# Rows of 64 tokens by two picks in the second table pass, and part of the one-hot work moved beside the last rows

## The chip, the cores and the metric

One core of one Trainium2 chip runs the kernel. The metric is the device time of one execution in microseconds (us). Three executions of the kernel before took 2889.9, 2887.84 and 2890.3 us, median 2889.9. Engines: TensorE (PE, and PEld for its weight loads), VectorE (DVE), ScalarE (ACT), GpSimd (POOL), SyncE (SP, which issues transfers only).

## The reference

Two transformer blocks over 256 tokens of width 2048, all in float32. The change touches only the last step of the second one, a product-key expert layer:

```
def peer_ffn(h, w_q, sub_keys, expert_u, expert_v):
    scores = einsum('bshpd,hpnd->bshpn', q, sub_keys)      # q = h @ w_q, 8 heads x 2 halves
    sv, si = top_k(scores, 16)                             # 16 best keys of each half
    cand = sv[..., 0, :, None] + sv[..., 1, None, :]       # 256 sums, of which the 16 best
    tv, tp = top_k(cand, 16)                               # name 16 experts of 16384
    eidx, gw = ..., softmax(tv)
    a = einsum('td,ted->te', x, expert_u[eidx])            # 128 dot products of each token
    a = gelu(a) * gw
    out = einsum('te,ted->td', a, expert_v[eidx])          # weighted sum of 128 rows
```

So each of the 256 tokens picks 8 x 16 = 128 experts, reads 128 rows of the first table (`expert_u`, 8 KB a row), and adds up 128 rows of the second (`expert_v`).

## The kernel before, in words

The tokens stand in two blocks of 128, one token per partition; `tk` is 0 or 1. One "row" of the kernel is one pick of all 128 tokens of a block: an indirect transfer by POOL (line 624) that brings 128 table rows, 1 MB, into one slot of SBUF. There are 256 of them, n = 0 to 127 for the first block and 128 to 255 for the second. This is the row stage.

**The row stage.** Rows land in the slots of `aring` (4) and `ring` (4); `ROW_SLOT` and `ROW_BEFORE` (lines 246 to 253) name each row's slot and the row that must have left it; from n = 128 on there are 8. POOL waits for that row (line 618 to 622) and issues the next. Most rows are dotted on DVE (`dot`, line 2692) with the tokens in `sq`. 47 rows are dotted on PE (`TURN_EARLY`, every 4th from 30 to 142; `TURN_LATE`, every 5th from 144 to 229): `turn_and_dot` transposes the row in 16 pieces into M (line 1283), ACT copies M to `acc` in two halves (`keep_row`, line 1767), and PE multiplies the copy by the turned tokens (line 1293). DVE reads the diagonal of the product (`read_diagonal`, line 2702); in its written order this stands behind the dot of row n + 8 for a late row n (`READ_BEHIND`), and DVE waits there if PE is not done. DVE also picks the experts in 57 parts spread between the dots (`PICK_AT`).

**The one-hot groups.** The upper half of `expert_v` is not gathered but read whole, in 64 blocks of 1 MB, and multiplied on PE by a dense matrix `mix[tk]` of coefficients (the dense stage, line 1331). `mix` is made in groups of 4 tokens, 32 groups for each block. For the first block ACT makes a group (`one_hots` in the ACT part, lines 1743, 1748, 1751: 8 + 1 + 4 instructions), PE multiplies (`spread_coefs`, line 1271) and ACT copies the product into `mix[0]` (`keep_mix`, line 1757). These 32 groups stand between the late PE rows: `spreads_after` gives 28 of them to the 18 rows 144 to 229, one or two behind each row, and the last row has four more. PE and ACT both run in this written order, so a late PE row does not start before the groups of the row ahead of it are through. For the second block the coefficients are ready only when all rows are dotted; `mix[1]` lies where `ring` and `aring` are. Its one-hots are made by DVE (`one_hots`, line 2730), weighed by ACT (line 1809), multiplied by PE and kept by ACT. Two are made ahead (`MARKED_AT`).

**The burst.** Behind row 255: gelu, coefficients, their transpose, then 32 groups of `mix[1]`, on DVE each followed by one `v_add`: the lower half of `expert_v` is gathered by POOL (line 636, 256 transfers of 0.5 MB) and added by DVE with the coefficient (line 2720), except 8 rows of `V_ON_PE` and the last 4 of `V_LAST_ON_PE`, which PE adds.

**The dense stage.** PE multiplies 64 blocks, each 8 products for two `tk` and two halves, loaded by SP into three buffers as PE frees them; beside it POOL and DVE go on with the gathered rows. DVE ends the first dense half at n = 242 (`DENSE_OUT`), the second at n = 254, and the gathered half last.

The functions that the diff touches, with the line numbers of the profile:

## Time and profile before

| | |
|---|---|
| Median of 3 runs | 2889.9 us (2887.84 to 2890.3) |
| Profiled execution: time, span | 2892.87 us, 2891.1 us |
| PE, DVE, ACT, POOL busy | 2627.9, 2138.4, 621.4, 911.1 us |
| Moved by the DMA engines | 935.10 MB, mean 323 GB/s |
| Mean granted TensorE clock | 0.948 of 2.4 GHz |

The profile shows one execution, taken by the hardware profiler. "Idle before" an instruction names what released it, inferred from semaphores. A line such as L1283 is that line of the kernel. In rows of transfers "DMA ring<-peer_u" is the wait for that transfer to land. Busy time of PE is modelled at its ends, and the busy time of POOL is rough.

### The profile page before, as it was taken

The page shows a single profiled execution, that of the slowest core. Times are in us where ns is not written, and L with a number is a line of the kernel's source. Part 1 is how long each engine was busy: PE and PEld are TensorE (multiplying, and loading weights), DVE is VectorE, ACT ScalarE, POOL GpSimd, SP SyncE. Part 2 cuts the span into 40 slices and gives each one's busy share as a digit, 9 for nine tenths or more (in the row PEclk, how much of TensorE's full clock was granted, in tenths as well). Part 3 has the DMA queues.
Part 4 walks back from the last instruction along what each step waited for, and adds up shares of the span by engine and source line. Part 5 has one row for each costly group of instructions (what it writes and reads, how often), then busy time and mean ns, then how long its engine had stood idle before and what let it go on. Part 6 is the DMA issues. An engine that isn't in the chain of part 4 may idle for free.

```text
span 2891.1 us, 30550 instructions
## 1 busy us (share of the span) xinstructions
PE 2627.9 (91%) x11608; PEld 2038.4 (71%) x11608; DVE 2138.4 (74%) x2836; ACT 621.4 (21%) x1328; POOL 911.1 (32%) x712
## 2 busy tenths in 40 slices
PE   7999999999999999999999998776676648999998
PEld 6888778855687787578657687666666635666665
DVE  6797476697896757425677778989999888656666
ACT  1121240300100210121000221221477765000000
POOL 1100001000010100000000036767677676666664
PEclk9999999999999999999999999888877759999999
DMA  9954469888787743325878789999999998999998
GB/s 403 421 223 146 175 241 411 352 305 348 277 336 302 292 145 136 142 102 222 347 274 321 278 352 417 421 421 415 413 421 412 399 352 296 408 415 414 413 414 357
DMA packets 147734, 935.10 MB, mean 323 GB/s; under 512 B 16400, under 2 KB 16656, under 8 KB 53136
## 3 DMA queue, kind: packets, MB, share of 16 engines
q0 software_dynamic: 101376, 604.02, 52.3%
q1 hardware_dynamic: 44784, 320.66, 28.6%
q10 hardware_dynamic: 1440, 8.59, 0.7%
q8 instruction: 88, 1.44, 0.2%
q14 instruction: 46, 0.38, 0.0%
HBM read 929.02 MB, written 4.19 MB: 323 GB/s over the span
## 4 chain that ended last, share of the span: by engine, by line
PE 67%; DVE 11%; DMA 9%; ACT 6%; POOL 4%; issue 3%; DVEq 0%; SPq 0%; POOLq 0%
PE G L652 30%; PE M L1331 14%; PE M L979 6%; DMA aring<-peer_u,proj 3%; PE B L979 3%; ACT vec L1743 2%; DVE aring L2692 2%; POOL ring L624 2%; PE M L1283 2%; PE G L979 2%; POOL aring L624 2%; DMA aring<-ada 1%; PE G L1271 1%; PE M L893 1%; ACT vec L1748 1%
## 5 line engine op out<-in xcount | busy, mean ns | idle before, releaser
L652 PE MATMUL G<-h,ring 128*128 128x256 f32 x2784 | 610.2, 380 | 0.0
L652 PEld LDWEIGHTS G<-h,ring 128*128 128x128 f32 x2784 | 527.4, 190 | 79.3 <-issue 6.7
L609 POOL DMA_DIRECT2D aring<-ada x176 | 93.1, 529 | 1445.5 <-DVE mods L1879 1399.9
L1879 DVE CUSTOM_DVE_ANT_0 aring<-aring,acc,vec 128x2048 f32<-128x2048 f32 x160 | 372.4, 2351 | 57.5 <-DMA aring<-ada 54.5
L652 PE MATMUL G<-proj,ring 128*128 128x256 f32 x1472 | 322.1, 380 | 1.0 <-DVE proj L2515 0.9
L652 PEld LDWEIGHTS G<-proj,ring 128*128 128x128 f32 x1472 | 279.7, 191 | 41.4 <-issue 3.2
L1331 PE MATMUL M<-sq,mix 128*128 128x512 f32 x688 | 301.6, 594 | 1.2 <-DMA sq<-v_blocks 1.2
L624 POOL DMA_INDIRECT aring<-peer_u,proj x131 | 229.9, 1755 | 155.8 <-DVE proj L2645 51.8
L2692 DVE CUSTOM_DVE_ANT_0 aring<-sq,aring 128x2048 f32<-128x2048 f32 x107 | 244.1, 2291 | 36.2 <-DMA aring<-peer_u,proj 35.0
L1331 PEld LDWEIGHTS M<-sq,mix 128*128 128x128 f32 x688 | 203.5, 297 | 91.0 <-DMA sq<-v_blocks 2.0
L2720 DVE SCALAR_TENSOR_TENSOR vec<-acc,dots,vec 128x1024 f32<-128x1024 f32 x147 | 188.9, 1285 | 96.0 <-DMA acc<-v_rows,proj 85.8
L636 POOL DMA_INDIRECT acc<-v_rows,proj x151 | 198.5, 1315 | 105.6 <-DVE vec L2720 77.0
L624 POOL DMA_INDIRECT ring<-peer_u,proj x108 | 199.9, 1851 | 74.1 <-DVE dots L2692 39.1
L2692 DVE CUSTOM_DVE_ANT_0 ring<-sq,ring 128x2048 f32<-128x2048 f32 x85 | 193.7, 2291 | 10.9 <-DMA ring<-peer_u,proj 6.9
L1381 ACT ACTIVATE proj<-G 128x256 f32<-128x256 f32 (+1 forms) x118 | 45.5, 386 | 584.8 <-PE G L652 499.2
L1767 ACT ACTIVATE acc<-M 128x1024 f32<-128x1024 f32 x94 | 94.9, 1024 | 267.5 <-PE M L1283 266.8
L1331 PE MATMUL M<-proj,mix 128*128 128x512 f32 x336 | 148.0, 593 | 1.0 <-DMA proj<-v_blocks 1.0
L1293 PE MATMUL B<-h,acc 128*128 128x128 f32 x928 | 126.2, 301 | 14.1 <-ACT acc L1767 12.7
L1271 PE MATMUL G<-vec 128*128 128x128 f32 x256 | 53.3, 373 | 92.4 <-ACT vec L1751 92.4
L1293 PEld LDWEIGHTS B<-h,acc 128*128 128x128 f32 x928 | 124.3, 219 | 17.0 <-issue 14.5
L1331 PEld LDWEIGHTS M<-proj,mix 128*128 128x128 f32 x336 | 99.7, 297 | 45.9 <-DMA proj<-v_blocks 1.7
L2720 DVE SCALAR_TENSOR_TENSOR vec<-mix,dots,vec 128x1024 f32<-128x1024 f32 x66 | 84.8, 1285 | 42.2 <-DMA mix<-v_rows,proj 39.0
(519 smaller groups left out, 3795.7 us busy)
## 6 DMA issues: line engine op xcount, KB each, us to landing
ring<-weights SPq DMA_DIRECT2D x217, 1024.0 KB, 6.6
aring<-ada POOLq DMA_DIRECT2D x176, 1024.0 KB, 9.2
sq<-v_blocks SPq DMA_DIRECT2D x43, 1024.0 KB
proj<-v_blocks SPq DMA_DIRECT2D x21, 1024.0 KB
ring<-first SPq DMA_DIRECT2D x16, 896.0 KB, 10.0
sq<-ada POOLq DMA_DIRECT2D x8, 1024.0 KB, 20.4
acc<-ada POOLq DMA_DIRECT2D x4, 1024.0 KB, 19.8
proj<-ada POOLq DMA_DIRECT2D x4, 1024.0 KB, 23.9
```

The costliest lines, as they stand in the source:

```text
L609: pool.dma_start(ada_at(n), ada[n]).then_inc(ada_in[ada_slot(n)], 16)
L624: pool.indirect_dma_start(u_slot(n), None, peer_u, where).then_inc(u_in[ROW_SLOT[n]], 16)
L636: pool.indirect_dma_start(v_slots[V_SLOT[n]], None, v_rows, where).then_inc(v_in[V_SLOT[n]], 16)
L652: mm = nc.tensor.matmul(bank[:, 0:TOK], lhsT=ring[:, slot, weights_at + t * P:weights_at + (t + 1) * P], rhs=rhs[:, t, :], start=(t == ord ...
L979: mm = nc.tensor.matmul(banks[n], lhsT=tokens, rhs=columns, start=(k == 0), stop=(k == 7))
L1271: mm = nc.tensor.matmul(G[n % 2][:, k * P:(k + 1) * P], lhsT=far[:, k * P:(k + 1) * P], rhs=near[:, k * P:(k + 1) * P], start=True, stop=True)
L1293: mm = nc.tensor.matmul(O[k % 2][:, 0:P], lhsT=turned_row[:, j * P:(j + 1) * P], rhs=tokens, start=(j == 0), stop=(j == DT - 1))
L1331: mm = nc.tensor.matmul(M[:, tk * HALF + half * 512:tk * HALF + (half + 1) * 512], lhsT=mix[tk][:, j // FREED, :, j % FREED], rhs=blocks[j ...
L1767: nc.scalar.activation(turned_row[:, half * 1024:(half + 1) * 1024], M[:, half * 1024:(half + 1) * 1024], ACT.Copy).then_inc(row_kept, 1)
L1879: V_.tensor_tensor_reduce(out=tile, in0=tile, in1=vector, scale=1.0, scalar=bias, op0=ALU.mult, op1=ALU.add, accum_out=column).then_inc(ad ...
L2692: V_.tensor_tensor_reduce(out=u_slot(n), in0=sq[:, tk * D:(tk + 1) * D], in1=u_slot(n), scale=1.0, scalar=0.0, op0=ALU.mult, op1=ALU.add, ...
L2720: V_.scalar_tensor_tensor(out=y, in0=v_slots[V_SLOT[n]], scalar=c, in1=y, op0=ALU.mult, op1=ALU.add).then_inc(v_added, 1)
```

## The change

The rows of the second block are laid out anew: a row brings two picks of 64 tokens, not one of 128. Tokens 0 to 63 of the second block are its first half, 64 to 127 the second; `HALF_ROWS` puts the eight sets of 16 rows in order so that the first half is through after six sets (row 223). For this SP copies the picks, the shares and two copies of the first half's tokens between partitions. The first half's coefficients are made at row 236, and ten of its 16 one-hot groups (`MARKED_AT`, `BESIDE_ROWS`) are made beside rows 226 to 254. `mix[1]` of the first half lies in slots 0, 2, 4 and 6, so rows from 222 on use slots 1, 3, 5, 7 and, from 228, `acc[:, 0]`. The first block's 32 groups now all stand behind PE rows 138 to 217 (17 rows), and late PE rows are 147 to 242 (20 rows). The picks of the second block are made by n = 197. The burst keeps 22 groups (`SECTION`), 22 `v_add` and 5 rows on PE.

```
 TURN_EARLY = range(30, 144, 4)
-TURN_LATE = range(144, 230, 5)
+TURN_LATE = range(147, 243, 5)
 FREE_BEHIND = 4
 READ_BEHIND = {n: n + (6 if n in TURN_EARLY else 8) for n in [*TURN_EARLY, *TURN_LATE]}
-EXP_AT = 212
+EXP_AT = 202
 PICKS_TURNED_AT = 28
-MARKED_AT = {248: 0, 252: 1}
+PAIR = P // 2
+HALF_ROWS = [(0, 0), (0, 1), (1, 0), (0, 2), (1, 1), (0, 3), (1, 2), (1, 3)]
+FIRST_HALF_DONE = NSLOT + 6 * SEL
+COEFS_AT, HALF_GELU_AT, HALF_COEFS_AT = NSLOT + 9, 232, 236
+LATE_START = NSLOT + 10
+NARROW, ACC_ROWS = 222, 228
+SPREADS_UNTIL = 217
+BESIDE_ROWS = {237: (0, 2), 242: (2, 10)}
+MARKED_AT = {226: 0, 230: 1, 240: 2, 242: 3, 244: 4, 246: 5, 248: 6, 250: 7, 252: 8, 254: 9}
+SECTION = range(len(MARKED_AT), P // 4)
 VSLOTS = 5
 LATE_SLOTS = 4
 LATE_FROM = 104
 FREED = 32
-V_ON_PE = [4 + 5 * i for i in range(8)]
+V_ON_PE = [4 + 5 * i for i in range(5)]
 V_LAST_ON_PE = [2 * NSLOT - 9 + 2 * i for i in range(4)]
-EARLY_DENSE = {8: 0, 12: 1, 16: 2, 20: 3, 24: 4, 28: 5, 25: 6, 29: 7}
+EARLY_DENSE = {4: 0, 8: 1, 9: 2, 12: 3, 13: 4, 16: 5, 17: 6, 20: 7}
 NAMED = [(0, 0, 1), (0, 1, 1), (0, 2, 2), (0, 4, 2), (0, 6, 2), (1, 0, 2), (1, 2, 2), (1, 4, 2), (1, 6, 2)]
 NAMED_BEFORE = {}
 for _tk, _hh, _n in NAMED:
     for _i in range(_n):
         NAMED_BEFORE[_tk * HEADS + _hh + _i] = len(NAMED_BEFORE) and max(NAMED_BEFORE.values()) + (_i == 0)
 PICK_PARTS = [(tk, hh, n, part) for tk, hh, n in NAMED for part in range(3 * n + 1)]
-PICK_AT = [*range(1, SEL, 2), *range(SEL, 104, 4), *range(104, 240, 5)][0:len(PICK_PARTS) - 4]
+PICK_AT = [*range(1, SEL, 2), *[SEL + 31 * i // 8 for i in range(31)], *[137 + 14 * i // 3 for i in range(14)]]
...
+    if _n >= NARROW:
+        _free = [1, 3, 5, 7] + [8] * (_n >= ACC_ROWS)
...
+def half_row(n):
+
+    half, group = HALF_ROWS[(n - NSLOT) // SEL]
+    return half, group, PAIR * half + SEL * group + n % SEL
+
+
+def dot_column(n):
+
+    return half_row(n)[2] if n >= NSLOT else n
...
+        half_tokens = [acc[:, 0, :], sq[:, D:2 * D]]
...
         def spreads_after(n):
 
-            late, beside = len(TURN_LATE), P // 4 - 4
-            i = pe_rows_before(n) - pe_rows_before(NSLOT + SEL)
-            return range(beside * i // late, beside * (i + 1) // late if i + 1 < late else P // 4)
+            rows = [m for m in PE_ROWS if LATE_START <= m <= SPREADS_UNTIL]
+            if n not in rows:
+                return range(0)
+            i = rows.index(n)
+            return range(P // 4 * i // len(rows), P // 4 * (i + 1) // len(rows))
...
+            if s == 8 and n >= NARROW:
+                return acc[:, 0, :]
...
+            lower, upper = slice(0, PAIR), slice(PAIR, P)
+
+            def by_halves(dst, src, groups, done):
+
+                for half in range(2):
+                    for u, rows in enumerate((lower, upper)):
+                        to = dst[rows, PAIR * half:PAIR * (half + 1)].rearrange("p (g k) -> p g k", k=SEL)
+                        sp.dma_start(to[:, groups, :], src[upper if half else lower, P:2 * P].rearrange(
+                            "p (g u k) -> p g u k", u=2, k=SEL)[:, groups, u, :]).then_inc(done, 16)
+
+            for g in range(4):
+                sp.wait_ge(picked, NAMED_BEFORE[HEADS + 2 * g] + 1)
+                by_halves(half_picks, picks, slice(g, g + 1), pairs_in)
+                if g == 0:
+                    for rows in (lower, upper):
+                        sp.dma_start(half_tokens[0][rows, :], sq[lower, D:2 * D]).then_inc(rows_in, 16)
+                    sp.wait_ge(rows_in, 16 + 32)
+                    sp.dma_start(sq[lower, D:2 * D], sq[upper, D:2 * D]).then_inc(rows_in, 16)
+            sp.wait_ge(picked, len(NAMED) + 1)
+            by_halves(half_gates, gate_w, slice(0, 4), shares_in)
...
+                elif n % SEL == 0:
+                    pool.wait_ge(pairs_in, 16 + 64 * (half_row(n)[1] + 1))
+                if n == ACC_ROWS:
+                    pool.wait_ge(dot_done, dve_rows_before(FIRST_HALF_DONE))
...
+                if n == 1:
+                    last = max(m for m in range(2 * NSLOT) if ROW_SLOT[m] == 8)
+                    if on_pe(last):
+                        pool.wait_ge(row_turned, 2 * pe_rows_before(last) + 2)
+                    else:
+                        pool.wait_ge(dot_done, dve_rows_before(last) + 1)
+                if n == 3:
...
+            def turn_half(half, groups_before):
+
+                pe.wait_ge(coef_ready, half + 2)
+                pe.wait_ge(mix_in, groups_before)
+                for u in range(2):
+                    rows = slice(PAIR * u, PAIR * (u + 1))
+                    mm = nc.tensor.matmul(G[1][rows, 0:PAIR], lhsT=half_coefs(half), rhs=ident[:, rows], start=True, stop=True)
+                mm.then_inc(turned, 1)
+
+            def turn_back():
+
+                pe.wait_ge(turned_kept, 5)
+                nc.tensor.transpose(M[:, HALF:HALF + P], kept_coef[:, P:2 * P], ident).then_inc(turned, 1)
...
-            for n in range(NSLOT + SEL, 2 * NSLOT):
+            rows_on_pe(7 * SEL, LATE_START)
+            turn_coefs()
+            for n in range(LATE_START, 2 * NSLOT):
                 if on_pe(n):
                     turn_and_dot(n)
+                    if n == HALF_GELU_AT:
+                        turn_half(0, P // 4)
+                    if n in BESIDE_ROWS:
+                        for g in range(*BESIDE_ROWS[n]):
+                            spread_coefs(1, g)
                     for g in spreads_after(n):
                         if g == PICKS_TURNED_AT:
                             turn_picks(1)
                         spread_coefs(0, g)
-            turn_coefs(1)
+            turn_half(1, P // 4 + len(MARKED_AT))
...
-            for g in range(P // 4):
+            for i, g in enumerate(SECTION):
                 spread_coefs(1, g)
-                if g % 4 >= 2:
-                    add_row(g // 4, g % 4 - 2)
-                if g in EARLY_DENSE:
-                    block_here(EARLY_DENSE[g] // 4)
-                    dense_rows(EARLY_DENSE[g] // 2, 0, [EARLY_DENSE[g] % 2])
+                if i % 4 >= 2:
+                    add_row(i // 4, i % 4 - 2)
+                if i in EARLY_DENSE:
+                    block_here(EARLY_DENSE[i] // 4)
+                    dense_rows(EARLY_DENSE[i] // 2, 0, [EARLY_DENSE[i] % 2])
+                if i == 10:
+                    turn_back()
+            pe.wait_ge(turned_kept, 6)
...
+                if tk == 1 and g == 0:
+                    act.wait_ge(dot_done, dve_rows_before(NARROW))
+                    act.wait_ge(row_turned, 2 * pe_rows_before(NARROW))
...
+                    if n == SPREADS_UNTIL:
+                        keep_mix(0, P // 4 - 1)
+                    if n == HALF_GELU_AT:
+                        dots_gelu(FIRST_HALF_DONE, half_coefs(0))
+                        keep_coefs(kept_coef[:, P:P + PAIR], 4)
+                        act.wait_ge(turned_kept, 4)
+                    if n in BESIDE_ROWS:
+                        for g in range(*BESIDE_ROWS[n]):
+                            weigh_hot(g)
+                            keep_mix(1, g)
                 if n == EXP_AT:
                     gate_exp(1)
-            keep_mix(0, P // 4 - 1)
             nc.scalar.activation(small[:, 10:11], eps, ACT.Gelu)
-            dots_gelu(1)
-            keep_coefs(1)
-
-            def weigh_hot(g):
-
-                act.wait_ge(hot_marked, g + 1)
-                far = hot[1][:, g % 2, 0, :]
-                for k in range(4):
-                    n = P + 4 * g + k
-                    ins = nc.scalar.activation(far[:, k * P:(k + 1) * P], far[:, k * P:(k + 1) * P], ACT.Copy,
-                                               scale=kept_coef[:, n:n + 1])
-                ins.then_inc(hot_weighed, 1)
+            dots_gelu(2 * NSLOT, half_coefs(1))
+            keep_coefs(kept_coef[:, P + PAIR:2 * P], 5)
...
+            weigh_hot(SECTION[0])
+            for i, g in enumerate(SECTION):
+                if i % 4 == 0 and i // 4 < len(V_ON_PE):
+                    make_diag(i // 4)
                 if g + 1 < P // 4:
                     weigh_hot(g + 1)
                 keep_mix(1, g)
+                if i == 11:
+                    keep_back()
...
+            def half_coefficients(half):
+
+                dve.wait_ge(gelu_done, half + 2)
+                dve.wait_ge(shares_in, 16 + 64)
+                d = half_coefs(half)
+                step(tt(d, d, half_gates[:, PAIR * half:PAIR * (half + 1)], ALU.mult), on=coef_ready)
...
-                    dve.wait_ge(ht_copied, 4)
+                    dve.wait_ge(rows_in, 16 + 32)
+                if n == NSLOT + 2 * SEL:
+                    dve.wait_ge(rows_in, 16 + 48)
...
-                if n == NSLOT + SEL - 1:
-                    coefficients(0)
+                if n == COEFS_AT:
+                    coefficients()
+                if n == HALF_COEFS_AT:
+                    half_coefficients(0)
                 if n in MARKED_AT:
                     dve.wait_ge(turned_kept, 3)
                     one_hots(MARKED_AT[n])
-            coefficients(1)
+            half_coefficients(1)
             dve.wait_ge(mix_in, P // 4)
-            in_burst = [n for n in range(P // 4 + len(V_ON_PE)) if n not in V_ON_PE]
-            for g in range(P // 4):
-                if g >= len(MARKED_AT):
-                    one_hots(g)
-                v_add(in_burst[g])
+            in_burst = [n for n in range(len(SECTION) + len(V_ON_PE)) if n not in V_ON_PE]
+            for i, g in enumerate(SECTION):
+                one_hots(g)
+                v_add(in_burst[i])
```

## Rows read from the trace of the kernel before

**Rows 1.** Windows by stage: length; busy us (count) of PE, PEld, DVE, ACT, POOL; clock; DMA; GB/s.

```profile
2070.00:2305.00 235.00, 160.40 (x1048) 153.54 (x1047) 212.76 (x323) 172.28 (x401) 168.14 (x92) 0.77 1.00 411
...
2356.00:2440.00 84.00, 65.12 (x306) 45.65 (x307) 74.46 (x64) 59.42 (x170) 57.00 (x41) 0.87 0.80 271
2440.00:2860.00 420.00, 419.04 (x976) 289.39 (x976) 260.57 (x206) 1.28 (x4) 265.97 (x206) 1.00 1.02 412
```

**Rows 2.** Chain that ended last, late PE rows: start us, us, engine and line.

```profile
2164.21 3.10 PE M L1283 x16
2168.36 2.34 ACT vec L1743 x8
2173.67 2.35 ACT vec L1743 x8
2178.55 2.07 PE G L1271 x8
2180.62 3.42 PE M L1283 x16
...
2197.36 3.43 PE M L1283 x16
...
2207.87 3.39 PE M L1283 x16
```

**Rows 3.** PE, in order of time: start, us, line, [idle before].

```profile
2058.03 1.91 PE L1283 MATMUL M<-cst,aring 128*128 128x128 f32 x16
...
2071.30 1.91 PE L1283 MATMUL M<-cst,ring 128*128 128x128 f32 x16
2073.59 3.81 PE L1293 MATMUL B<-sq,acc 128*128 128x128 f32 x32 [0.38 <-ACT acc L1767]
```

**Rows 4.** The same of the last late rows, and the groups behind them.

```profile
2287.82 1.91 PE L1283 MATMUL M<-cst,aring 128*128 128x128 f32 x16
...
2302.88 3.62 PE L1283 MATMUL M<-cst,ring 128*128 128x128 f32 x16
...
2317.75 2.08 PE L1271 MATMUL G<-vec 128*128 128x128 f32 x8 [4.16 <-ACT vec L1751]
...
2325.55 2.08 PE L1271 MATMUL G<-vec 128*128 128x128 f32 x8 [5.30 <-ACT vec L1751]
```

**Rows 5.** ACT by line from 2080 to 2345 us: busy, mean ns, idle before.

```profile
L1767 ACT ACTIVATE acc<-M 128x1024 f32<-128x1024 f32 x34 | 34.6, 1025 | 59.5 <-PE M L1283 58.8 <-issue 0.7
```

**Rows 6.** DVE and POOL late in the row stage.

```profile
2276.79 2.29 DVE L2692 CUSTOM_DVE_ANT_0 aring<-sq,aring 128x2048 f32<-128x2048 f32 x1 [2.67 <-DMA aring<-peer_u,proj]
...
2289.22 2.29 DVE L2692 CUSTOM_DVE_ANT_0 aring<-sq,aring 128x2048 f32<-128x2048 f32 x1 [1.68 <-DMA aring<-peer_u,proj]
...
2307.28 2.42 POOL L624 DMA_INDIRECT ring<-peer_u,proj  x1 [5.01 <-PE M L1283]
...
2310.30 0.29 DVE L2702 CUSTOM_DVE_ANT_0 att<-B,cst 128x128 f32<-128x128 f32 x1 [1.41 <-PE B L1293]
...
2314.94 2.29 DVE L2692 CUSTOM_DVE_ANT_0 ring<-sq,ring 128x2048 f32<-128x2048 f32 x1
...
2353.41 2.29 DVE L2692 CUSTOM_DVE_ANT_0 aring<-sq,aring 128x2048 f32<-128x2048 f32 x1 [0.21 <-DMA aring<-peer_u,proj]
```

**Rows 7.** DVE in the burst.

```profile
2383.91 1.22 DVE L2730 TENSOR_TENSOR proj<-cst 128x1024 f32<-128x1024 f32 x1
...
2386.29 1.21 DVE L2730 TENSOR_TENSOR proj<-cst 128x1024 f32<-128x1024 f32 x1
```

**Rows 8.** ACT's last copy of the burst; the end of the kernel.

```profile
2439.15 0.60 ACT L1757 ACTIVATE mix<-G 128x512 f32<-128x512 f32 x1 [0.77 <-PE G L1271]
...
2865.45 1.23 DVE L2779 TENSOR_TENSOR vec<-M,att 128x1024 f32<-128x1024 f32 x1 [4.25 <-PE M L1331]
...
2872.11 3.60 PE L1331 MATMUL M<-sq,mix 128*128 128x512 f32 x8
...
2886.82 1.22 DVE L2774 TENSOR_TENSOR x<-x,vec 128x1024 f32<-128x1024 f32 x1
```

More of the change, by code:

```diff
@@ L2598, in _ @@
             masked = tile(37)
-            spare = powers[:, :, :, :].rearrange("p a b c -> p (a b c)")
             gsum = small[:, 112:128]
@@ L2623, in name_experts @@
                 here = slice(at, at + picks_n)
[L2624 to L2625 removed]
+                by_name = [small[:, a:a + 2 * picks_n] for a in (16, 128)]
+                names, half = [a.rearrange("p (s m) -> p s m", s=2) for a in by_name]
                 half_i = by_name[1].bitcast(U32)
[L2627 to L2628 removed]
+                number = small[:, 80:80 + picks_n]
+                if tk == 0:
+                    room = flat(proj[:, 0:2 * n, :])
+                else:
+                    room = scores[1][:, 256 * (hh - 2):256 * (hh + 2)] if hh else acc[:, 0, 0:1024]
                 marks = room.rearrange("p (s m j) -> p s m j", s=2, j=SEL)
```

113 lines of the change are left out of this document (68 added, 45 removed).

## The prediction

> **What bounds the kernel now.** I read the windows by stage first, then the chain of waits through the late PE rows, then PE, DVE and POOL in order of time around the places that the change touches. The windows show three stages [rows 1]. From 2070 to 2305 us, the late rows, the DMA engines have a share of 1.00, so the row stage looks bound by transfers: 85 rows, from 144 to 229, in about 214 us, 2.5 us each. From 2356 to 2440, the burst, they have 0.80 and move 271 GB/s: something else sets the pace. From 2440 to 2860, the dense stage, PE is busy 419 of 420 us and the DMA engines are full too, 412 GB/s: two resources are at their end together.
>
> The chain shows what the windows hide [rows 2]. Through the late rows it goes from PE to ACT and back and hardly touches a transfer: transposes of a row, keep, then per group 5.31 us from one start of L1743 to the next (2168.36 to 2173.67), then the next row. A row with two groups behind it takes 16.4 us (2164.21 to 2180.62) or 16.7 (to 2197.36), one with a single group 10.5 (to 2207.87). So a row itself costs 5 to 6 us of this serial chain (ACT waits for PE's transposes 59.5 us in all over it [rows 5]) and a group 5.3. Rows of this kind come every 5 x 2.5 = 12.5 us. The kernel before gives 28 groups to 18 rows. From row 144 (2071.30; it is the last one before the first L1293 that reads `sq`, which only rows from 144 do [rows 3]) to row 229 (2302.88 [rows 4]) the chain takes 231.6 us for 17 steps with 26 groups, 13.6 a step: 1.1 us too slow each. It starts with no delay and ends about 16 us late. That is just what the order allows: at row 237 DVE waits 1.41 us for PE, and POOL 5.01 us for a slot that PE holds [rows 6]. The chain PE-ACT is thus as tight as the transfers, and has no reserve left.
>
> **The change part by part.** Sums are against the profiled execution: span 2891.1 us, time 2892.87; the median of three is 2889.9, 3.0 below, and I take that off at the end.
>
> 1. The first block's groups. All 32 now stand behind 17 rows, 138 to 217. Written out, 15 rows carry two groups, 138 and one in the middle (177) one each. From the start of row 138 to that of row 217 there are 16 steps: 14 of two groups at 16.4 and 2 of one at 10.7 (10.5 to 10.8): 251 us. Turning and keeping the picks before group 28 adds 2.5 (the step 2317.75 to 2325.55 is 7.8 us, not 5.3 [rows 4]), and the Exp of the shares, which stands in this chain too, 0 to 2 (an estimate from one transpose-and-keep like the picks'; I take 1.6). Together 255 us. Transfers would bring the same 79 rows in 79 x 2.5 = 198 us. The excess is 57 us, and only the 13 to 16 us by which PE may be late is free. Row 138 starts on PE at 2058.03 [rows 3], 4 us later after the change (part 3): row 217 at 2317, and its product ends 7.4 later (as row 229's, 2302.88 to 2310.30 [rows 4, 6]), at 2324.5. DVE may not pass row 225 before. It dots row 225 from 2276.79 to 2279 now (counted back from the last dot, row 255's at 2353.41, PE rows left out) [rows 6]. Shift there: 45 us.
>
> 2. Behind row 217. Row 222 has two groups ahead of it: PE starts it at 2333.5 and has left its slot 3.7 later. Since rows from 222 on have slots 1, 3, 5, 7 alone, and `acc` from 228, the slot of 222 is that of row 230: POOL waits for it until 2337. A row takes 7.7 us from issue to dot (row 240: 2307.28 to 2314.94), so row 230 is dotted at 2344.5 where it was at 2289.22 [rows 6]: shift 55. Then 26 rows to the end, 66.4 us now. With 4 or 5 slots a slot's round is 7.7 + 2.3 + 0.3 = 10.3 us, so 2.1 to 2.6 a row. DVE has 23 dots at 2.2, nine one-hots at 1.2 and the reads: 63 us. I take 2.6 a row, 68 us, +2; the ends are -2 (2.49 a row) and +17 (3.2, if the two PE rows in it hold slots as well). The last row then ends 57 us later than now.
>
> 3. SP's copies. Two transfers of 0.5 MB (tokens), a third behind them, and 20 small ones. 1.6 MB at 411 GB/s is 4 us of the DMA engines, taken before row 138. The small ones have no like here; they move 0.13 MB, so their floor is nothing; their ceiling, at the pace of one whole row each, is 20 x 2.5 = 50 us, but they fall where the chain of part 1 binds and the DMA engines have 20% to spare; I take 0 to 6, and 0. POOL needs the pairs of picks 8 rows ahead of DVE: names at rows 105, 132, 165, 197 for issues 128, 144, 176, 208, 3 rows or more ahead of need, with up to 7 rows in flight behind: nothing.
>
> The Trainium skill, page "DMA: Bandwidth & Descriptors", section Bandwidth, says that transfers under 64 KB are dominated by their descriptors and gives 0.68 us of engine time for 4 KB: by it the 20 small ones would cost up to 14 us if nothing hid them. Its section "Why small descriptors are slow (HBM only)" takes this back between parts of SBUF. No row here shows either, and the sum stands without them.
>
> 4. Picks made earlier on DVE. The parts are the same, 53 of them up to row 197 instead of up to 239. Between rows 144 and 197 DVE has four dots of 2.2, one read of 0.3 and 1.07 parts of some 2.7 us in 12.5 us: it fits (12.0), and DVE is held by PE there anyhow. 0; if it does not fit, 1 to 3.
>
> 5. The burst. 32 groups fill 2356 to 2439.15 [rows 8], at 2.38 us each on DVE (2383.91 to 2386.29: one-hots and a `v_add`) [rows 7] plus 7 us of waits at its head. Ten fewer: -23.8. Group 9's marking lies before the last dot, so its weighing, product and copy, 4.5 us, end 2.3 us behind that dot, and the gelu comes after them: +2.3. The turn back of the coefficients (one transpose, one copy) lies beside DVE's work: 0. The dense stage starts 21.5 us earlier relative to the last row.
>
> 6. What the dense stage gives back. Ten `v_add` and three PE rows have left the burst: 13 transfers of 0.52 MB must run later, in a stage whose DMA engines are full (412 GB/s [rows 1]): 16.5 us. They are not all lost: at 2865.45 DVE waits 4.25 us for PE [rows 8], and this goes, because PE is now earlier than the gathered rows. Net of parts 5 and 6: -21.5 + 16.5 - 4 = -9. The check by bytes: the burst leaves 35% of 412 GB/s unused for 84 us, 29 us of transfers; 62 us of it leave 21: -8. Bounds: -21.5 (if the rows ride along free) and -5.
>
> Sum: +57 - 9 = +48. With the span's 2891 that is 2939 and a time of 2941; less 3.0, **2938 us**. The terms that could be too large are the step of 16.4 us and the slots' round; both have more room below than above, so I forecast **2935 us**.
>
> **The rivals.**
> (a) The rows ride over it: the delay of PE is absorbed, the row stage stays bound by transfers, and the burst's gain is kept: 2889.9 + 4 - 9, so 2885; with the full 21.5, 2872. For it: the DMA share of 1.00 before, and that ACT is busy 172 of 235 us. Against: the waits at row 237, and that busy ACT is not free ACT in a serial chain.
> (b) TensorE's clock. It is granted 0.77 over the late rows [rows 1]; at the level of 2.4 GHz the 16 transposes take 1.91 us, at 1.2 GHz 3.1 to 3.6 [rows 2, 4]. If it stayed high the steps of two groups would be 15.1 us (2287.82 to 2302.88 [rows 4]): 14 x 1.3 less: 2917. Against: before each second group PE has stood idle 4.16 us or so [rows 4], and there are more such now. The Trainium skill, "TensorE: Matmul & The Clock Gate", section "HAM oscillation — how this bites in real kernels", says the clock falls back when PE pauses for others; by that rule this rival fails.
> (c) Few slots: 3.2 us a row behind row 230, part 2's upper end: 2950. For it: four slots and PE holding one of them.
> (d) The ten groups do not get done beside the rows: ACT comes late to row 242 after part 1's delay, and the burst waits for them; 10 x 2.4 is then not saved: 2958. Against: ACT has only one row in five to keep there.
>
> **How the numbers follow.** The chain of parts 1 and 2 binds in full: 0.64, by itself 2918 to 2955. (b) 0.12. (c) and (d) 0.08. (a) 0.12, and some middle, a partly absorbed delay that the burst just pays for, 0.04. Slower is the likeliest by far: the forecast, (b), (c), (d), 0.84; same 0.04; faster 0.12. Two measurements of this kernel can be told apart from 0.2%, about 6 us. The range of 8 in 10 leaves out (a) and the upper tail: 2900 to 2956.
>
> **What would show it.** Right: the stage from row 138 to 217 has DMA shares of 0.75 to 0.85 and some 330 to 350 GB/s; late PE rows start every 16 us; DVE waits for PE at its diagonal reads (L2702's successor), 30 us or more in sum; the last dot comes at 2400 or later; the burst takes 60 to 64 us; PE ends the last block before DVE has added the gathered rows. Wrong: the DMA share stays at 1.00 through the rows and the last dot lies at 2360, or the burst's gain is over 20 us at the end of the kernel. The forecast stands on the step of 16.4 us and on the order of PE and ACT as written; if the steps with two groups are shorter than 14, it falls.

## The result

| | before | after |
|---|---|---|
| Median (runs) | 2889.9 us (2887.84 to 2890.3) | 2956.41 us (2953.29 to 2958.55) |
| Profiled execution: time, span | 2892.87, 2891.1 us | 2957.94, 2956.1 us |
| PE, DVE, ACT, POOL busy | 2627.9, 2138.4, 621.4, 911.1 us | 2640.2, 2137.9, 624.7, 876.7 us |
| Mean DMA rate, granted clock | 323 GB/s, 0.948 | 317 GB/s, 0.941 |

Against runs of the kernel before on the same chip the ratio is 1.0227, 95% interval [1.0209, 1.0245]: 66 us slower, between 60 and 71. The forecast was 2935 and slower; the direction and the mechanism held, and the loss is 21 us larger than predicted. The median lies 0.4 us above the upper end of the range.

### Where the time went

Windows by stage of the changed kernel (length; busy us and count of PE, PEld, DVE, ACT, POOL; clock; DMA share; GB/s). The first two are from the row stage, the third holds the rows beside which the ten groups are made, the fourth the burst, the fifth the dense stage:

```profile
1780.00:2055.00 275.00, 179.86 (x1218) 172.14 (x1218) 245.38 (x442) 52.44 (x53) 184.34 (x103) 0.82 0.99 400
2055.00:2325.00 270.00, 168.28 (x1090) 160.22 (x1091) 211.70 (x324) 198.37 (x462) 148.07 (x89) 0.75 0.89 353
2325.00:2430.00 105.00, 61.11 (x383) 57.25 (x381) 73.22 (x76) 42.51 (x93) 58.79 (x36) 0.70 0.87 326
2430.00:2490.00 60.00, 48.18 (x230) 32.80 (x231) 54.47 (x49) 42.78 (x124) 43.91 (x28) 0.92 0.82 270
2490.00:2900.00 410.00, 409.93 (x955) 283.18 (x955) 253.24 (x200) 0.00 (x0) 254.04 (x201) 1.00 1.02 412
```

And the same windows of the kernel before, for the first two:

```profile
1780.00:2055.00 275.00, 187.70 (x1272) 180.44 (x1272) 256.55 (x447) 60.15 (x61) 203.15 (x111) 0.83 1.01 420
2055.00:2325.00 270.00, 182.50 (x1216) 174.26 (x1214) 242.10 (x357) 193.32 (x448) 191.36 (x105) 0.78 1.00 410
```

Read DMA and GB/s from top to bottom. The late rows were a stage with full DMA engines; now they move 353 GB/s, and no engine is near full: DVE has 212 of 270 us, ACT 198, PE 168. Where nothing is full, an order of work may be what binds, and the chain of waits shows which. It is that of [rows 2], through more of the stage (start us, us, engine and line; L1359 the transposes, L1874 their copies, L1837 the one-hots, L1347 the groups' products):

```profile
2163.91 3.38 PE M L1359 x16
2167.31 1.02 ACT acc L1874
2168.34 2.34 ACT vec L1837 x8
...
2173.64 2.35 ACT vec L1837 x8
...
2178.53 2.08 PE G L1347 x8
2180.60 3.43 PE M L1359 x16
...
2197.34 3.43 PE M L1359 x16
...
2207.84 3.10 PE M L1359 x16
```

16.7 us (2163.91 to 2180.60, and the next, to 2197.34) with two groups behind the row, 10.5 with one (to 2207.84): the steps of the kernel before. There they were 13.6 us in the mean for a row that comes every 12.5 us; now the mean is 15.7. PE's rows in order of time (start, us, line, [idle before]), from row 138, the first with a group, to row 217, the last:

```profile
2074.25 1.91 PE L1359 MATMUL M<-cst,aring 128*128 128x128 f32 x16
...
2306.03 2.41 PE L1359 MATMUL M<-cst,aring 128*128 128x128 f32 x16
...
2323.41 2.08 PE L1347 MATMUL G<-vec 128*128 128x128 f32 x8 [3.23 <-ACT vec L1845]
2325.27 3.01 PE L1359 MATMUL M<-cst,aring 128*128 128x128 f32 x16
```

16 steps in 251.0 us for 79 rows that the transfers could bring in 198. What PE holds back is told by POOL and DVE at row 225, whose slot is row 217's (POOL first, then DVE with row 225 and row 230):

```profile
2328.56 0.94 POOL L680 DMA_INDIRECT aring<-peer_u,powers  x1 [16.20 <-PE M L1359]
```

```profile
2334.11 2.29 DVE L2812 CUSTOM_DVE_ANT_0 aring<-sq,aring 128x2048 f32<-128x2048 f32 x1 [12.26 <-DMA aring<-peer_u,powers]
...
2352.73 2.29 DVE L2812 CUSTOM_DVE_ANT_0 aring<-sq,aring 128x2048 f32<-128x2048 f32 x1 [5.44 <-DMA aring<-peer_u,powers]
```

DVE's wait is named after a transfer, but the transfer was issued late because POOL had stood 16.20 us at a slot that PE had not read: behind a "<-DMA" look for what the issue waited for. Over 1780 to 2430 us the waits sum to this (engine and line, for whom: us, times, longest):

```profile
POOL aring L680 <- PE M L1359: 94.4, 13, 16.2
POOL aring L680 <- DVE dots L2812: 60.1, 16, 16.4
...
DVE att L2822 <- PE B L1372: 32.6, 8, 7.7
```

Row 225 is 57 us later than before (2276.79 in [rows 6]), row 230 63.5 us (2289.22), the last dot 75.2 us (2353.41), here with the last copy of the burst on ACT and the end:

```profile
2428.59 2.28 DVE L2812 CUSTOM_DVE_ANT_0 aring<-sq,aring 128x2048 f32<-128x2048 f32 x1
```

```profile
2487.15 0.60 ACT L1854 ACTIVATE mix<-G 128x512 f32<-128x512 f32 x1 [0.77 <-PE G L1347]
```

```profile
2941.50 1.98 PE L1459 MATMUL B<-mix,proj 128*128 128x512 f32 x4 [0.64 <-DMA mix<-v_rows,proj]
2944.06 1.98 PE L1459 MATMUL B<-proj 128*128 128x512 f32 x4 [0.57 <-DMA proj<-v_rows,proj]
...
2951.88 1.23 DVE L2904 TENSOR_TENSOR x<-x,vec 128x1024 f32<-128x1024 f32 x1
```

So the burst lasts 58.6 us (last dot to last copy) where it lasted 85.7, 27 less; the rest up to the last instruction 464.7 where it was 447.7 ([rows 8]), 17 more. Only 10 us of the shortening arrive at the end. The last gathered rows now wait for transfers, where before PE was last and DVE waited 4.25 us for it [rows 8]; PE, which adds the last of them (L1459), waits for them too. Of the chain that ended last, from 2490 us on, these transfers are 67%; before, from 2440 on, 91% was PE's products.

### The profile page after: what moved, and what is told of

It reads as the page before. It is cut to its first block, busy times and chain, and to the rows that moved or that the text cites. A ratio compares the mean times of both kernels' runs of the same rounds, so it can differ in the third digit from the quotient of the medians.

```text
span 2956.1 us, 30796 instructions
## 1 busy us (share of the span) xinstructions
PE 2640.2 (89%) x11700; PEld 2050.4 (69%) x11700; DVE 2137.9 (72%) x2844; ACT 624.7 (21%) x1332; POOL 876.7 (30%) x712
## 4 chain that ended last, share of the span: by engine, by line
PE 48%; DMA 22%; DVE 15%; ACT 7%; POOL 5%; issue 4%; DVEq 0%; SPq 0%; ACTq 0%; POOLq 0%
PE G L714 26%; DMA acc<-v_rows,proj 7%; PE M L1041 6%; DMA aring<-ada 5%; PE B L1041 3%; DMA mix<-v_rows,proj 3%; DVE aring L2812 3%; ACT vec L1837 3%; DMA aring<-peer_u,proj 2%; DVE vec L2847 2%; PE M L1359 2%; POOL acc L698 2%; DVE aring L1987 2%; PE G L1041 2%; DMA aring<-peer_u,powers 1%
## 5 line engine op out<-in xcount | busy, mean ns | idle before, releaser
L2812 DVE CUSTOM_DVE_ANT_0 aring<-sq,aring 128x2048 f32<-128x2048 f32 x82 | 186.7, 2289 | 48.4 <-DMA aring<-peer_u,powers 28.3
L680 POOL DMA_INDIRECT aring<-peer_u,proj x67 | 123.0, 1835 | 138.6 <-DVE dots L2812 72.8
L1874 ACT ACTIVATE acc<-M 128x1024 f32<-128x1024 f32 x98 | 98.8, 1024 | 290.8 <-PE M L1359 290.8
L680 POOL DMA_INDIRECT aring<-peer_u,powers x61 | 111.1, 1821 | 130.4 <-PE M L1359 94.1
L1347 PE MATMUL G<-vec 128*128 128x128 f32 x256 | 54.6, 379 | 97.0 <-ACT vec L1845 97.0
L1372 PE MATMUL B<-h,acc 128*128 128x128 f32 x864 | 116.3, 299 | 22.9 <-DVE dots L2822 11.6
L2812 DVE CUSTOM_DVE_ANT_0 ring<-sq,ring 128x2048 f32<-128x2048 f32 x53 | 121.1, 2291 | 16.8 <-DMA ring<-peer_u,powers 9.9
L1372 PEld LDWEIGHTS B<-h,acc 128*128 128x128 f32 x864 | 114.0, 216 | 26.2 <-issue 12.9
L1347 PEld LDWEIGHTS G<-vec 128*128 128x128 f32 x256 | 46.2, 271 | 103.8 <-ACT vec L1845 103.8
```

What stands on the lines that cost most here:

```text
L680: pool.indirect_dma_start(u_slot(n), None, peer_u, where).then_inc(u_in[ROW_SLOT[n]], 16)
L1347: mm = nc.tensor.matmul(G[n % 2][:, k * P:(k + 1) * P], lhsT=far[:, k * P:(k + 1) * P], rhs=near[:, k * P:(k + 1) * P], start=True, stop=True)
L1372: mm = nc.tensor.matmul(O[k % 2][:, 0:P], lhsT=turned_row[:, j * P:(j + 1) * P], rhs=tokens, start=(j == 0), stop=(j == DT - 1))
L1874: nc.scalar.activation(turned_row[:, half * 1024:(half + 1) * 1024], M[:, half * 1024:(half + 1) * 1024], ACT.Copy).then_inc(row_kept, 1)
L2812: V_.tensor_tensor_reduce(out=u_slot(n), in0=tokens, in1=u_slot(n), scale=1.0, scalar=0.0, op0=ALU.mult, op1=ALU.add, accum_out=dots[:, 0, ...
```

## The experiments

Each edit is to the kernel named, and "..." stands for lines that are not shown. Differences in us are taken from the ratios to the kernel before on the same chip, with 2890 for it; "last dot" and "row n" are starts in the profiled execution. "After" is the changed kernel.

### The serial chain

**before_packed**: in the kernel before, all 32 groups behind the 17 rows 144 to 224, as many as the change uses.

```
-            late, beside = len(TURN_LATE), P // 4 - 4
-            i = pe_rows_before(n) - pe_rows_before(NSLOT + SEL)
-            return range(beside * i // late, beside * (i + 1) // late if i + 1 < late else P // 4)
+            rows = [m for m in PE_ROWS if NSLOT + SEL <= m <= 224]
+            if n not in rows:
+                return range(0)
+            i = rows.index(n)
+            return range(P // 4 * i // len(rows), P // 4 * (i + 1) // len(rows))
```

> The kernel before, with one thing of the change alone: the first block's 32 one-hot groups stand behind 17 late PE rows (144 to 224, 1.88 each) instead of 28 behind 18 rows and four behind the last. No new layout, no copies, no narrow slots, the burst as before. Theory (the serial chain PE-ACT binds: 5.5 us a row and 5.35 us a group): 14 steps of 16.4 us and 2 of 10.7 from row 144 at 2071 us, so row 224's product ends near 2334, and DVE, which waits there at row 232, is 37 to 40 us late: 2927 to 2932 us. Rival (the row stage is bound by transfers and PE's delay is absorbed; what the change lost came from its copies and its few slots): 2890 us.

Measured 2927.34 us (2924.74 to 2928.94), ratio 1.0138 [1.0121, 1.0155]: +40. The last dot is at 2388.62, 35 us late. Late rows, from 2070 to 2305 us, and the last diagonal read behind a row of two groups (row 224), on DVE:

```profile
2070.00:2305.00 235.00, 148.83 (x939) 141.77 (x937) 191.79 (x292) 178.23 (x423) 133.13 (x80) 0.73 0.92 368
```

```profile
2331.30 0.29 DVE L2704 CUSTOM_DVE_ANT_0 att<-B,cst 128x128 f32<-128x128 f32 x1 [9.59 <-PE B L1295]
```

Nothing else of the change is in this kernel. From row 144 to row 229 PE now has 32 groups to do where it had 26: the six that stood behind row 229 stand ahead of it. At 5.3 us each they are 32 us, the last dot is 35 late, and the kernel 40 us slower, 35 to 45. Rival (a) falls.

**after_light_hots**: after, each first-block group with two first ACT instructions (L1837) and not eight; the one-hots of the others are left out.

```
                 for s in range(2):
-                    for k in range(4):
-                        ins = nc.scalar.activation(both[:, s, k * P:(k + 1) * P], C("iota_keys"), ACT.Abs,
-                                                   bias=kept_idx(s, 4 * g + k), scale=-1.0)
+                    ins = nc.scalar.activation(both[:, s, 0:P], C("iota_keys"), ACT.Abs,
+                                               bias=kept_idx(s, 4 * g), scale=-1.0)
```

> The changed kernel, in which ACT makes a one-hot group of the first block with 2 instead of 8 instructions of the first kind (the other six are left out, so those one-hots are not made); all waits and the order stay. A group is then some 3.2 us on ACT and a step with two groups 12.3 us, no more than five rows of transfers (12.5). Theory: the chain no longer binds, some 41 to 45 us go, 2908 to 2916 us; what is left over the kernel before is the early delay and the slots. Rival: ACT's work on the groups was not the cause, over 2945 us.

Measured 2914.31 us (2910.29 to 2917.16), ratio 1.009 [1.0073, 1.0107]: 40 us less than after, as expected. Row 217 starts on PE at 2272.6, not 2325.3, the last dot at 2384.54. The window and POOL's waits from 1940 to 2430 us (here the 94 us for PE are gone, and what is left is DVE):

```profile
2070.00:2305.00 235.00, 174.13 (x1202) 164.85 (x1202) 207.34 (x315) 153.41 (x300) 168.88 (x92) 0.85 1.00 409
```

```profile
POOL aring L680 <- DVE dots L2811: 54.3, 12, 17.2
POOL ring L680 <- DVE dots L2811: 47.4, 13, 6.2
```

In after ACT was busy 198 of 270 us and still, in turn with PE, set the pace. Taking work from it gives the DMA engines their full share back: that the chain binds is shown from both sides. The other 26 us of the loss are not the chain's.

**after_until_227**: the groups end ten rows later, and the picks two groups earlier.

```
-SPREADS_UNTIL = 217
+SPREADS_UNTIL = 227
-PICKS_TURNED_AT = 28
+PICKS_TURNED_AT = 26
```

> The changed kernel with its 32 groups of the first block behind 19 rows, 138 to 227, instead of 17, 138 to 217 (1.68 a row), and the picks turned before group 26. Theory (chain of 5.5 us a row and 5.35 a group): from row 138 to the start of row 227, 18 steps with 30 groups, 260 us; DVE may pass row 235 at 2074 + 260 + 10 = 2344 us, where it stood at 2368 in the trace after: 16 to 24 us faster, 2932 to 2940 us. Rival (the groups' work costs its time wherever it stands): 2953 to 2957 us.

Measured 2936.71 us (2935.27 to 2939.34), ratio 1.0163 [1.0147, 1.0178]: 18 less than after; last dot 2409.18. A new wait shows that the order can't simply be loosened: the first half's coefficients at row 236 need a gelu that stands on ACT behind the late rows. DVE, there (in after the same instruction, at 2373.81, waits for nothing):

```profile
2358.13 0.23 DVE L2835 TENSOR_TENSOR dots<-dots,powers 128x64 f32<-128x64 f32 x1 [9.18 <-ACT dots L1818]
```

### Ahead of row 138

The prediction let the chain start at 2062; it starts at 2074.25. Two causes are seen in the trace of after. DVE waits for the Exp of the first block's shares, then POOL for DVE. The DVE row of after, and that of before:

```profile
1948.48 0.29 DVE L2779 TENSOR_REDUCE small<-proj 128x8 f32<-128x128 f32 x1 [13.41 <-ACT proj L1809]
```

```profile
1949.36 0.29 DVE L2660 TENSOR_REDUCE small<-proj 128x8 f32<-128x128 f32 x1 [5.11 <-ACT proj L1721]
```

**after_exp_early**: the Exp stands 16 rows earlier in ACT's order.

```
-            rows_on_pe(0, 6 * SEL)
+            rows_on_pe(0, 5 * SEL)
             gate_exp(0)
-            rows_on_pe(6 * SEL, 7 * SEL)
+            rows_on_pe(5 * SEL, 7 * SEL)
```

> The changed kernel, with ACT's Exp of the first block's shares behind PE rows below 80 instead of below 96. In the trace after, DVE stands idle 13.4 us at row 90 for this Exp, because the picks are now made earlier and the Exp is not. Theory: the delay goes through to the chain's start, and 8 to 13 us go: 2943 to 2948 us. Rival: the slots or the chain absorb it, under 3 us: 2953 to 2957.

Measured 2951.63 us (2951.14 to 2954.42), ratio 1.0223 [1.0206, 1.024]. The wait is gone, row 138 starts at 2067.75 (6.5 earlier) and the last dot at 2421.2 (7.4 earlier). The medians differ by 5 us, the ratios by 1, with intervals of 5 either way: the expected gain of 8 to 13 is missed, and in the time the effect is not settled. It is seen in the rows alone. Single traces differ here too: in the four kernels that are the same up to row 138 (after, after_light_hots, after_until_227, after_no_beside) it starts between 2074.25 and 2078.01, and in the kernel before and its five variants between 2056.39 and 2061.05. The early Exp lies 6.5 us below the lowest of the four.

**after_no_copies**: the three copies of tokens by SP (0.5 MB each) are left out, the 20 small ones stay.

```
-                    for rows in (lower, upper):
-                        sp.dma_start(half_tokens[0][rows, :], sq[lower, D:2 * D]).then_inc(rows_in, 16)
-                    sp.wait_ge(rows_in, 16 + 32)
-                    sp.dma_start(sq[lower, D:2 * D], sq[upper, D:2 * D]).then_inc(rows_in, 16)
+                    pass
...
-                    dve.wait_ge(rows_in, 16 + 32)
-                if n == NSLOT + 2 * SEL:
-                    dve.wait_ge(rows_in, 16 + 48)
+                    dve.wait_ge(ht_copied, 4)
```

> The changed kernel without SP's three copies of the tokens between partitions (the picks and shares are still copied; the dots of the second block's rows then meet tokens that are not theirs, so the copies are left out of the computation). In the trace after, the DMA engines move 302 to 368 GB/s at full share for 34 us around these copies, and row 138 starts on PE 16 us later than before, of which the run with the early Exp gave back 6. Theory: the copies cost 6 to 10 us, which the chain passes on: 2946 to 2950 us. Rival: the delay is DVE's (picks made earlier) and not the copies': 2954 to 2957 us.

Measured 2950.84 us (2945.04 to 2954.39), just above the range expected, ratio 1.0204 [1.0187, 1.0221]: 6.6 less than after by the ratios, but the intervals overlap, so the time alone does not settle this either. Row 138 is 7.8 us and the last dot 7.2 us earlier; of that 3.5 us are left in the span of the profiled execution, whose burst is 4.6 us longer. In the DMA queues of after from 1990 to 2020 us (packets, MB, share of the 16 engines), q1 carries the copies and four small transfers:

```profile
q0 software_dynamic: 1134, 8.26, 78.7%
q1 hardware_dynamic: 560, 1.59, 22.7%
```

and without the copies, the small ones alone:

```profile
q0 software_dynamic: 1717, 12.50, 100.5%
q1 hardware_dynamic: 320, 0.02, 0.7%
```

22.0% of 30 us is 6.6 us for 1.57 MB, 238 GB/s: a copy between partitions takes the engines 1.7 times as long per byte as the reads at 412 GB/s with which I priced it (4 us). The small ones in this window, 4 KB each (16 of the 20 are; the four with the shares have 16 KB), take 0.7% of 30 us, 0.2 us for four: 0.05 us each of all 16 engines, which is 0.84 us of a single one (320 packets for the four, 10.5 ns each). The Trainium skill gives 0.68 us for 4 KB ("DMA: Bandwidth & Descriptors", section Bandwidth), as the span in which such a transfer from HBM is busy. The prediction took that as time of all the engines together, and so came to 14 us for 20; the trace shows that this reading is far too high, and does not contradict the figure itself. Nor does the trace bear out the page's section "Why small descriptors are slow (HBM only)", by which small pieces carry no penalty inside SBUF: 4 KB in 0.05 us of all engines is some 78 GB/s, a third of what the large copies reach.

### Slots and the ten groups

**before_narrow**: in the kernel before, rows from 222 on use slots 1, 3, 5, 7, and from 228 `acc` too.

```
+    if _n >= 222:
+        _free = [1, 3, 5, 7] + [0] * (_n >= 228)
```

> The kernel before, with the slots of the change alone: rows from 222 use slots 1, 3, 5, 7 and from 228 one more (slot 0). Theory: with 4 or 5 slots a row takes 2.6 to 3 us and PE's rows hold slots, 8 to 18 us slower over 34 rows: 2898 to 2908 us. Rival (a slot's round of 10 us is covered by four slots): 2890 to 2892 us.

Measured 2904.76 us (2900.9 to 2907.33), ratio 1.0057 [1.004, 1.0074]: +16, as expected. The last dot is at 2363.94, 10.5 us late, and the profiled span 11.3 us longer; the ratio's interval begins at 12. With four slots POOL waits for PE at row 226, 9.90 us: a slot held by a PE row is now a quarter of all. Later, at 2341 to 2346 us, DVE takes a row each 2.5 us: there five slots carry full pace; the loss was made earlier, with four slots and PE in one of them.

**after_no_beside**: after, with eight slots to the end, no groups beside the rows and a burst of 32.

```
-NARROW, ACC_ROWS = 222, 228
+NARROW, ACC_ROWS = 256, 256
-BESIDE_ROWS = {237: (0, 2), 242: (2, 10)}
-MARKED_AT = {226: 0, 230: 1, 240: 2, 242: 3, 244: 4, 246: 5, 248: 6, 250: 7, 252: 8, 254: 9}
-V_ON_PE = [4 + 5 * i for i in range(5)]
+BESIDE_ROWS = {}
+MARKED_AT = {}
+V_ON_PE = [4 + 5 * i for i in range(8)]
...
             half_coefficients(1)
+            dve.wait_ge(turned_kept, 3)
```

(`EARLY_DENSE` is again that of the kernel before.)

> The changed kernel with the groups of the first block ended by row 217 and everything of its rows as it is, but no second-block group made beside the last rows: eight slots to the end, a burst of 32 groups with eight V rows on PE, as before the change. Theory (late by PE's chain, 57 us or so, of which the eight slots take back what the narrow ones cost, and the burst's gain of 9 to 10 goes): the last dot 12 to 18 us earlier than the changed kernel's 2428.6, so 2411 to 2417, from there to the end the 534 of before, the time 2944 to 2952: the two parts of the second half of the change nearly cancel. Rival (the ten groups beside the rows cost nothing, and the slots neither): the last dot at 2428, the time 2963 to 2966. Rival (the slots were the greater loss): below 2940.

Measured 2949.01 us (2947.77 to 2953.18), ratio 1.0199 [1.0181, 1.0218]: 8 less than after, within the range expected; the two intervals leave anything from 1 to 15. The last dot and the end:

```profile
2409.86 2.29 DVE L2812 CUSTOM_DVE_ANT_0 ring<-sq,ring 128x2048 f32<-128x2048 f32 x1 [0.18 <-DMA ring<-peer_u,powers]
...
2944.17 1.23 DVE L2905 TENSOR_TENSOR x<-x,vec 128x1024 f32<-128x1024 f32 x1
```

The last dot is 18.7 us earlier than in after, and from there to the last instruction it takes 534.3 us, not 523.3. So the second half of the change costs 18.7 us ahead of the last dot and brings 11 behind it. It loses 8 us with the rest as it is. In the kernel before, where nothing else is wrong, the slots alone cost 16 us (before_narrow), and a burst without the ten groups brings 13 at most (before_short_burst, next).

### The burst and the dense stage

**before_short_burst**: the kernel before with a burst of 22 groups.

```
-V_ON_PE = [4 + 5 * i for i in range(8)]
+V_ON_PE = [4 + 5 * i for i in range(5)]
+BURST = 22
...
-            for g in range(P // 4):
+            for g in range(BURST):
...
+                if tk == 1 and g + 10 >= BURST:
+                    nc.scalar.activation(mix[tk][:, :, 4 * (g + 10):4 * (g + 10) + 4, :],
+                                         G[g % 2][:, :].rearrange("p (t a j) -> p a t j", t=4, a=P // FREED), ACT.Copy)
```

The other lines carry the 22 through the loops and waits, and set `EARLY_DENSE` as in after.

> The kernel before with a burst of 22 groups and five V rows added on PE, as in the changed kernel; the work of the last ten groups (marks, weighing, products) is left out, and their part of mix is a copy of groups 12 to 21 (ten ACT copies more). Nothing is changed ahead of the last dot, so it must stay at 2353. Theory (the dense stage gives back what the short burst does not transfer: thirteen V rows move into a stage whose DMA engines are full): 9 to 10 us faster at the end, 2879 to 2883, with the burst itself 20 to 24 us shorter. Rival (the rows ride along free behind the dense stage): 21 to 24 us, 2866 to 2869. Rival (ACT's copies and the queue take it all back): 2888 to 2891.

Measured 2879.75 us (2877.34 to 2885.06), ratio 0.9956 [0.994, 0.9972]: 13 us faster, 8 to 17. The profiled execution: the last dot, ACT's last copy of the burst, DVE's last instruction:

```profile
2356.28 2.28 DVE L2696 CUSTOM_DVE_ANT_0 aring<-sq,aring 128x2048 f32<-128x2048 f32 x1
```

```profile
2414.41 0.59 ACT L1761 ACTIVATE mix<-G 128x512 f32<-128x512 f32 x1
```

```profile
2879.00 1.22 DVE L2778 TENSOR_TENSOR x<-x,vec 128x1024 f32<-128x1024 f32 x1
```

A burst of 58.1 us, then 464.6 to the end: within half a microsecond what after shows (58.6, 464.7), against 85.7 and 447.7 with 32 groups. 27.6 us go and 16.9 come back, so 10.7 arrive. This is the most that ten groups can bring, with their work left out altogether. The burst shrank by more than the 20 to 24 us expected: ten groups at 2.38 us are 24, and two waits of DVE for PE's products at the head, 3.5 us in the kernel before, are 0.6 us in after.

**before_fewer_pe**: the late PE rows every sixth row and not every fifth, 15 and not 18.

```
-TURN_LATE = range(144, 230, 5)
+TURN_LATE = range(144, 230, 6)
```

> The kernel before, with late PE rows every 6th (15) instead of every 5th (18), the same 28 groups behind them. The chain has three rows less (16 us), DVE three dots more (6 us). Theory: the row stage loses some 5 us of transfers to PE's delay at present (411 instead of 421 GB/s over 235 us), and this comes back: 2884 to 2888 us. Rival: DVE, busy 19.5 of 20 us up to row 214, binds instead: 2890 to 2896 us.

Measured 2886.61 us (2884.41 to 2889.89, 11 runs), ratio 0.9984 [0.9975, 0.9993]: 5 us faster than before (2 to 7), as expected, and the only version with all the work in it that beats both. The chain has 3 rows less of 5 to 6 us, and the transfers their full rate, 419 GB/s where it was 411 [rows 1]:

```profile
2070.00:2305.00 235.00, 149.72 (x961) 142.61 (x959) 221.24 (x328) 174.00 (x413) 179.96 (x95) 0.75 1.01 419
```

**before_more_adds_on_pe**: that kernel with sixteen gathered rows added on PE in the burst, so that more transfers run there.

```
-V_ON_PE = [4 + 5 * i for i in range(8)]
+V_ON_PE = [2 + 3 * i for i in range(16)]
```

> The kernel before with its late PE rows every sixth row (15 of them, as in before_fewer_pe, 2886.6) and sixteen instead of eight gathered V rows added on PE in the burst, by a diagonal that ACT makes. The burst leaves some 29 us of DMA time unused, and eight more rows are 10 us of transfers (8 x 2.5 divided by two halves of 0.52 MB each, 1.27 us: 10.2 us) that the dense stage, full of transfers, no longer has. Theory (dense stage bound by DMA): 4 to 9 us faster than before_fewer_pe, 2877 to 2883. Rival (PE and ACT become the bound of the burst, 32 products with 16 adds): the burst grows by what is saved, 2884 to 2892. Rival (transfers in the burst are held by slots and not by adders): no change, 2886.

Measured 2894.63 us (2891.84 to 2900.9), ratio 1.0014 [1.0004, 1.0024]: 9 us slower than before_fewer_pe, so a miss, slower even than its worst rival. From the last dot to the last copy of the burst it takes 94.5 us, not 82.7, and from there to the end 446.2, not 447.6. Eight rows fewer in the dense stage save 1.3 us and not 10, since DVE now waits there for PE (before_fewer_pe waits 4.46 us at this place):

```profile
2866.64 1.23 DVE L2778 TENSOR_TENSOR vec<-M,att 128x1024 f32<-128x1024 f32 x1 [15.82 <-PE M L1331]
```

The dense stage has two floors close together: PE's, about 446 us, and that of the transfers, 464.6 with 13 rows more and some 443 in the kernel before (an estimate: its 447.7 less the wait of 4.25). The kernel before stands near the point where they meet. So fewer rows ahead of the stage cost nearly their full price, and more bring nothing. That price was higher than reckoned, about 1.6 us a row and not 1.27: 13 rows are 17.1 us and the 4.25 that DVE no longer waits, and the eight rows here are 1.3 us and a wait longer by 11.4.

**after_repaired**: after with the Exp early, the groups until 227 and all eight slots until row 236.

```
-NARROW, ACC_ROWS = 222, 228
+NARROW, ACC_ROWS = 236, 236
```

> The changed kernel with three repairs: Exp early, groups until row 227, and the few slots only from row 236 (instead of 222), 14 rows later. Theory (the costs add up as parts of one path): 5 for the Exp, 16 to 24 for the groups, 5 to 8 of the 16 us that few slots cost in the kernel before: 2920 to 2930 us, still slower than the kernel before, since the chain and the copies are left and the burst gives only 10. Rival (the parts lie beside each other and only the largest counts): 2932 to 2940 us.

Measured 2932.99 us (2924.58 to 2934.22, three executions; a fourth, of 14576 us, is left out), ratio 1.0134 [1.0112, 1.0157]: 27 less than after, 39 more than before. This is a miss: above the 2920 to 2930 that stood for costs that add up, and in the range of the rival, by which the parts lie beside each other. It beats after_until_227, its largest part, by 8 us, with intervals that overlap. Part of what was lost is seen: the wait for the gelu, new in after_until_227, has grown:

```profile
2353.25 0.23 DVE L2835 TENSOR_TENSOR dots<-dots,powers 128x64 f32<-128x64 f32 x1 [13.26 <-ACT dots L1818]
```

In ACT's order the gelu stands behind PE row 232, which starts at 2347.0 behind two groups. In both runs that moved the groups, something that the second block needs soon stood behind them.

## Why the prediction was right, and where it fell short

**Part 1, the chain: right.** The 16 steps take 251.0 us, as worked out without the extras; the 13 plain steps with two groups are 16.3 us in the mean, for 16.4. For those I allowed 4: the picks are there (19.2 us from 2306.03 to 2325.27), and a few shorter steps gave them back. That the chain makes the larger part of the loss, 40 of 66 us, is shown by before_packed, which adds it alone, and by after_light_hots, which takes it away. The DMA share over the chain's own stretch, 2075 to 2325 us, is 0.88 at 350 GB/s: the rate at the edge of the 330 to 350 that I named, the share above the 0.75 to 0.85. Of the other signs, the diagonal reads wait 32.6 us for PE (30 or more) and the last dot comes after 2400, but the burst takes 58.6 us and not 60 to 64.

**What was mis-sized.** The loss is 21 us larger than forecast, and 18 of them lie ahead of the last dot (75.2 us late and not 57). Another 3 are the step from the sum, 2938, to 2935, which I took because the slots' round and the step seemed to have more room below; the slots' round had it above. (1) The start of the chain: "4 us later" was 16 us. The Exp (6.5 us in the rows) and the copies (7.8 and not 4) are seen there; the 2 us that are left are less than what the same start differs by from one trace to the next. Part 4 of the prediction put the earlier picks at 0 because they fit on DVE; they do, but the Exp that they need did not move with them. (2) The hand-over at row 225: shift 57 and not 45. 8.3 of these 12 us are the later PE start (less the extras), the rest comes because row 225 is not only behind row 217 in DVE's order but in its slot, so that a whole transfer lies between. (3) Behind row 230, the term that weighs most in the end: 78.1 us to the end of the last dot and not 68, 3.0 us a row for 2.6 (rival c, 3.2, in part). after_no_beside shows what slots and groups cost together, 18.7 us, where part 2 has 12 (from 45 to 57). Row 230 itself was 63.5 late, not 55, which is (1) again.

**Parts 5 and 6, the burst: right in sum, by luck.** 27.2 us shorter where I had 21.5, and 17.1 given back where I had 12.5 (16.5 - 4): net -10 for -9, because two errors of about 5 us cancel. The burst lost waits at its head that I had not counted as part of the gain. And the term of -4 brought nothing: DVE's wait for PE is gone, but the rows cost 1.6 us each and not 1.27, which takes it back. before_short_burst shows the same two numbers with nothing else changed.

**Rivals.** (a) was wrong: the delay is not absorbed. (b) was wrong: the granted clock fell from 0.78 to 0.75 over 2055 to 2325 us and did not rise; in after_light_hots, where PE is busy 189 us of that stretch and not 168, it is 0.83. The Trainium skill says that the clock falls back when PE pauses to wait, there for transfers ("TensorE: Matmul & The Clock Gate", section "HAM oscillation — how this bites in real kernels"); both traces agree, with ACT as what PE waits for. (c) was partly right, with a price between mine and its own. (d) was wrong: the ten groups are made beside the rows, and the burst has 58.6 us; but it named a time, 2958, that the real sum reached by other terms. That its time lies nearer the measured one than mine is luck.

**How the parts add.** before_packed 35.2 us at the last dot, the groups' end seven rows earlier (224 to 217; 7 x 2.5 = 17.5), the slots and groups at the end 18.7, a start 3 us later than row 144's in before: 74.4 of 75.2. Only the first and third of these are from runs; the second is worked out, though after_until_227 (ten rows later, 18 us) speaks for it. That the sum fits to 1 us is better than single traces allow, whose starts differ by up to 4 to 5 us.

## What to carry to other kernels

Where two engines hand work to and fro in a written order, add up the time of one step and compare it with the time that the other resource gives it; neither engine's busy share shows that they are at their end (ACT 198 of 270 us here), and a queue that already runs a few us late before a change has no reserve for it. When a stage is to be shortened, ask what ran beside it for nothing: here 27 us of burst carried the transfers of 13 rows, which cost 17 us in the next stage. Before work is moved earlier, list all that it consumes (the Exp here), and who else uses its buffers.

## What the runs showed of the hardware

- Copies of 0.5 MB between partitions of SBUF took 6.6 us of all 16 DMA engines for 1.57 MB (238 GB/s, beside reads at 412 to 421), and landed 14.1 and 9.1 us after issue; the core's total fell to 302 GB/s over 10 us at a share of 1.00. A full DMA share is not a full rate.
- Transfers of 4 KB inside SBUF took some 0.05 us of all 16 engines each (0.84 us of one), but 6 to 9.5 us to land between rows of 1 MB: their price is the delay.
